# Gated scan with span products on rounded operands in two parts; delta inputs, gates and head norm in one block

## The reference

```
odn_x = _deltanet_scans(_dn_inputs(px[0], px[2], px[3], ...), _dn_inputs(pc[0], pc[2], pc[3], ...), ctx_out)
ohg_x = _hgrn2_scans(_hg_inputs(column-major px[4], px[5], px[6], lb), _hg_inputs(pc[4], pc[5], pc[6], lb), ctx_out)

def _dn_inputs(qkv, b, a, conv_w, a_log, dt_bias):
    qkv = silu(_short_conv(qkv, conv_w))
    q, k, v = split(qkv, 3)                      # 4 heads of 128 each
    q = _l2norm(q) * 128 ** -0.5 ; k = _l2norm(k)
    beta = sigmoid(b)
    g = -exp(a_log) * softplus(a + dt_bias)

gla_chunked, for each head and direction d, in chunks:
    gcum = cumsum(log_f)
    s_new = s * exp(g_last) + (k * exp(g_last - gcum))^T v
    att[i, j] = sum_k q[i, k] k[j, k] exp(gcum[i, k] - gcum[j, k])   for j <= i
    o = (q * exp(gcum)) s + att v
```

## Time and profile before

| quantity | value |
| --- | --- |
| device time, median of 3 (range) | 3605.03 us (3597.1 to 3607.6) |
| device time of the profiled execution | 3603.17 us |
| its span, first to last instruction | 3601.3 us |
| mean granted TensorE clock | 0.960 of 2.4 GHz |
| TensorE matmul busy | 3322.1 us (92%) |
| VectorE / ScalarE / GpSimd busy | 2266.4 / 1464.2 / 317.2 us |
| delta inputs, gates, head norm | 1955.3 to 2123.3 us of the span |
| gated scan | 2507.7 to 2661.3 us of the span |

### The profile page before, as it was taken

How to read it: one execution, slowest core, us unless ns; L and a number is a source line. 1 busy time by engine, 2 the same in 40 slices (tenths; PEclk the granted TensorE clock), 3 DMA queues, 4 the chain that set the end, 5 groups by cost and what they waited for, 6 DMA issues and landing times. The chain is left out here.

```text
span 3601.3 us, 46913 instructions
## 1 busy us (share of the span) xinstructions
PE 3322.1 (92%) x18718; PEld 2706.7 (75%) x18718; DVE 2266.4 (63%) x2960; ACT 1464.2 (41%) x1943; POOL 317.2 (9%) x213
## 2 busy tenths in 40 slices
PE   7998989999999998899998978889889989999996
PEld 5887678888887887777777858779667766777774
DVE  6467756656565237668686445665655337888885
ACT  5216713212123127533233333433333136777774
POOL 0020000000000000000000023411100012222221
PEclk8999989999999999999999979999989979999998
DMA  6540013443443211155652139012023258999993
GB/s 237 201 151 13 1 47 106 144 159 117 162 126 92 63 66 42 35 157 184 204 186 86 57 107 271 4 48 59 1 58 86 65 203 302 381 370 368 379 360 105
DMA packets 371768, 522.49 MB, mean 145 GB/s; under 512 B 19712, under 2 KB 313216, under 8 KB 345984
## 3 DMA queue, kind: packets, MB, share of 16 engines
q1 hardware_dynamic: 362112, 503.21, 41.8%
q0 software_dynamic: 9472, 16.80, 1.4%
HBM read 484.81 MB, written 51.90 MB: 149 GB/s over the span
## 5 line engine op out<-in xcount | busy, mean ns | idle before, releaser
L270 DVE TENSOR_TENSOR lo<-exp_raw,exp_hi 128x2048 fp32r<-128x2048 f32 x192 | 439.1, 2291 | 63.2 <-ACT exp_hi L3396 63.1
L3396 ACT CAST exp_hi<-exp_raw 128x2048 fp32r<-128x2048 f32 x192 | 366.5, 1913 | 112.7 <-PE exp_down_acc L265 50.7
L263 PE MATMUL ffn_acc<-normed_hi,up_w_hi 128*128 128x512 f32 (+1 forms) x1056 | 378.1, 358 | 9.6 <-DVE lo L626 6.1
L264 PE MATMUL ffn_acc<-lo,up_w_hi 128*128 128x512 f32 (+1 forms) x1056 | 377.9, 358 | 0.0
L263 PEld LDWEIGHTS ffn_acc<-normed_hi,up_w_hi 128*128 128x128 f32 x1056 | 199.9, 189 | 43.7 <-issue 6.7
L421 DVE SCALAR_TENSOR_TENSOR aside_w<-aside_w,aside_c 128x1024 f32<-128x1024 f32 x176 | 209.1, 1221 | 26.4 <-DMA aside_w<-in_ada_t 19.4
L264 PEld LDWEIGHTS ffn_acc<-lo,up_w_hi 128*128 128x128 f32 x1056 | 200.5, 190 | 32.1
L263 PE MATMUL ffn_acc<-gated_hi,down_w_hi 128*128 128x512 f32 (+1 forms) x528 | 190.8, 361 | 16.7 <-DVE lo L270 16.6
L1275 ACT ACTIVATE conv<-ffn_acc,vecs 128x768 f32<-128x768 f32 (+1 forms) x88 | 73.2, 882 | 292.6 <-PE ffn_acc L265 292.6
L265 PE MATMUL ffn_acc<-normed_hi,up_w_lo 128*128 128x512 f32 (+1 forms) x528 | 190.1, 360 | 0.0
L264 PE MATMUL ffn_acc<-lo,down_w_hi 128*128 128x512 f32 (+1 forms) x528 | 189.6, 359 | 0.0
(11 more groups left out here) (593 smaller groups left out, 8783.3 us busy)
## 6 DMA issues: line engine op xcount, KB each, us to landing
exp_raw<-in_w_experts SPq DMA_DIRECT2D x192, 1024.0 KB, 7.9
aside_w<-in_ada_t SPq DMA_DIRECT2D x176, 512.0 KB, 6.2
up_w<-in_ffn_up SPq DMA_DIRECT2D x88, 512.0 KB, 5.2
x_rows<-dn_zero SPq DMA_DIRECT2D x42, 384.0 KB, 5.3
y_rows<-dn_zero SPq DMA_DIRECT2D x42, 384.0 KB, 5.2
ada_w<-in_ada_first SPq DMA_DIRECT2D x8, 1024.0 KB, 12.1
v<-in_ada_t SPq DMA_DIRECT2D x16, 512.0 KB, 6.6
down_w<-in_ffn_down SPq DMA_DIRECT2D x16, 512.0 KB, 4.1
```

The source lines that it names most:

```text
L263: nc.tensor.matmul(out, left[0], right[0], start=start, stop=False)
L264: nc.tensor.matmul(out, left[0], right[1], start=False, stop=False)
L270: return engine.tensor_tensor(lo, value, hi.bitcast(F32), ALU.subtract)
L3396: nc.scalar.copy(hi[slot(e, j)][:], raw[tile(e, j)][:]).then_inc(tile_hi[j], 1)
```

## The change

**Delta inputs.** `dn_gates` and the call of `head_norm` for the delta inputs are gone; `dn_inputs` holds all three. TensorE makes chunks 0 to 7 (q and k), then the 48 products of the gates as a thirteenth item (n = 8) in the same ring of PSUM banks, then the chunks of v (n = 9 to 12). The sums of squares stand after the gates (chunks 0 to 3) and after n = 9 (4 to 7). The spreads of the roots stand inside n = 11 and n = 12 (0, 1, 2) and behind them (3 to 7). ScalarE's squares, exp, ln, sigmoid and root, and VectorE's reciprocal and scalings, stand between the steps of the chunks.

**Gated scan.** Each latent log gate is split into a rounded high part and a rounded rest. The high part lies in the context columns of `x` (two buffers), the rest over the gate in `fi`. Each span product, and each latent sum, is two `fp32r` matmuls in place of one float32 matmul. The tables are rounded once by GpSimd, `strict` by VectorE. The first head's gates are split at the end of `gated_rows` by VectorE; the next head's by a ScalarE copy ahead of the late exponentials, and a VectorE subtraction after level 1. Context sums stay float32.

```
+        sq = K.sb(ctx, "hn_sq", [P, HEADS, TT])
+        rstd = K.sb(ctx, "hn_rstd", [normed, TT])
+        root_hi = K.sb(ctx, "hn_root_hi", [normed, TT], FR)
+        root_lo = K.lo(rstd)
+        unit = K.sb(ctx, "hn_rows", [normed, normed], FR)
...
+        def bank(c):
+            return acc[:, {4: 1, 5: 2, 7: 1}[c]] if c in (4, 5, 7) else spread
...
+            def wide(n, between={}):
+                ring.begin(pe, n)
                 for c in range(KD):
...
+                    for a, b in parts:
+                        last = products(nc, acc[:, n % ACCS, a:b], ring.weights(n, c), right(c, a, b), c == 0, c == KD - 1)
+                    if c in between:
+                        stretch(between[c])
+                last.then_inc(ring.acc_full[n % ACCS], 1)
+            def gates():
+                pe.wait_ge(w_split, 1)
+                pe.wait_ge(ring.acc_free[gates_at % ACCS], gates_at // ACCS)
+                for a, b in parts:
+                    for c in range(KD):
+                        last = products(nc, acc[0:16, gates_at % ACCS, a:b], (wh[:, c, :], wl[:, c, :]), right(c, a, b),
+                                        c == 0, c == KD - 1)
+                last.then_inc(ring.acc_full[gates_at % ACCS], 1)
+            def turn_gates():
+                pe.wait_ge(rows_ready, 1)
+                for t in range(NT):
+                    last = nc.tensor.transpose(acc[:, gates_at % ACCS, TT + t * 16:TT + (t + 1) * 16], rows[:, t * P:(t + 1) * P], ident[0:16, 0:16])
+                last.then_inc(turned, 1)
+            def sums(some):
+                for c in some:
+                    pe.wait_ge(sq_full, c + 1)
+                    for a, b in parts:
+                        last = nc.tensor.matmul(spread[0:normed, a:b], pick[:, KD - 1 - c:KD - 1 - c + normed], sq[:, c % HEADS, a:b],
+                                                start=(c == 0), stop=(c == normed - 1))
+                    last.then_inc(summed, 1)
...
+            def stretch(c):
+                if c == 0:
+                    pe.wait_ge(split, 1)
+                elif c in (4, 5):
+                    pe.wait_ge(ring.acc_free[c - 3], (count + c - 4) // ACCS)
+                else:
+                    pe.wait_ge(scaled, {6: 4, 7: 5}.get(c, c))
+                row = unit[:, c:c + 1].broadcast_to([normed, P])
+                for a, b in parts:
+                    nc.tensor.matmul(bank(c)[:, a:b], row, root_hi[:, a:b], start=True, stop=False)
+                    last = nc.tensor.matmul(bank(c)[:, a:b], row, root_lo[:, a:b], start=False, stop=True)
+                last.then_inc(spread_full, 1)
+            ring.multiply(pe, acc, normed, first.ready, right, parts, inner_root)
+            gates()
+            pe.wait_ge(kept, 1)
+            sums(range(0, HEADS))
+            turn_gates()
+            wide(9)
+            sums(range(HEADS, normed))
+            wide(10)
+            wide(11, {5: 0})
+            wide(12, {1: 1, 5: 2})
+            for c in range(3, normed):
+                stretch(c)
...
+            def square(c):
+                if c >= HEADS:
+                    act.wait_ge(summed, c - HEADS + 1)
+                act.wait_ge(out[c % 2], c // 2 + 1)
+                nc.scalar.activation(sq[:, c % HEADS, :], dst[:, c, :], ACT.Square).then_inc(sq_full, 1)
...
+                if n == gates_at:
+                    for c in range(HEADS, normed):
+                        square(c)
+                    ring.high(act, n + 2)
+                    act.wait_ge(biased, 1)
+                    nc.scalar.activation(e[:], e[:], ACT.Exp)
+                    nc.scalar.activation(rate[:], K.row("a_log"), ACT.Exp)
+                    act.drain()
+                    nc.scalar.activation(l[:], e[:], ACT.Ln, bias=1.0)
+                    nc.scalar.activation(beta[:], beta[:], ACT.Sigmoid)
+                    act.drain()
+                    act.sem_inc(exped, 1)
...
+                if 1 <= n <= HEADS:
+                    square(n - 1)
+                if n == gates_at + 1:
+                    act.wait_ge(inverted, 1)
+                    nc.scalar.activation(rstd[:], rstd[:], ACT.Sqrt).then_inc(rooted, 1)
...
+            def take_gates():
+                ring.done(dve, gates_at)
+                nc.vector.tensor_copy(rows[:], acc[0:16, gates_at % ACCS, 0:TT]).then_inc(rows_ready, 1)
...
+            def bias_gates():
+                dve.wait_ge(turned, 1)
+                found = acc[:, gates_at % ACCS, TT:TT + NT * 16].rearrange("p (t n) -> p t n", n=16)
+                nc.vector.tensor_copy(beta[:], found[:, :, 0:8])
...
+            def scale(c):
+                dve.wait_ge(spread_full, c + 1)
+                nc.vector.scalar_tensor_tensor(dst[:, c, :], dst[:, c, :], P ** -0.5 if c < HEADS else 1.0,
+                                               bank(c)[:, 0:TT], ALU.mult, ALU.mult).then_inc(scaled, 1)
...
+            for n in range(count):
+                c = chunk[n]
+                if n == gates_at:
+                    take_gates()
+                    ring.low(dve, n + 2)
+                    bias_gates()
+                    continue
+                dve.wait_ge(mid[c % 2], c // 2 + 1)
...
+                if 4 <= n + 2 < count and n + 2 != gates_at:
+                    ring.low(dve, n + 2)
+                keep(n)
+                if n == gates_at + 1:
+                    dve.wait_ge(summed, normed)
+                    nc.vector.tensor_scalar(rstd[:], spread[0:normed, 0:TT], 1.0, EPS, ALU.mult, ALU.add)
+                    dve.drain()
+                    nc.vector.reciprocal(rstd[:], rstd[:]).then_inc(inverted, 1)
+                    finish_gates()
+                    dve.wait_ge(rooted, 1)
+                    nc.vector.tensor_copy(root_hi[:], rstd[:])
+                    dve.drain()
+                    lo_of(nc.vector, root_lo[:], rstd[:], root_hi[:]).then_inc(split, 1)
+                if n == gates_at + 2:
+                    scale(0)
+                    scale(1)
+                if n == gates_at + 3:
+                    scale(2)
+                    scale(3)
+            for c in range(4, normed):
+                scale(c)
+            dve.drain()
@@ gated_rows
+            def split_gates():
+                raw, hi, lo = gates
+                dve.wait_ge(unshifted, HEADS * P // G + 1)
+                nc.vector.tensor_copy(hi, raw).then_inc(gates_hi, 1)
+                dve.wait_ge(gates_hi, 1)
+                lo_of(nc.vector, lo, raw, hi)
...
             unshift(GATES - 1)
+            split_gates()
...
+def gate_parts(K, fi):
+    wide = lambda t, it: t[:, 0:NTX, 0:2 * HEADS * P].rearrange("p t (d h n) -> p t d h n", d=2, h=HEADS)[:, :, :, it, :]
+    own = lambda t, u: t[:, u * NTX:(u + 1) * NTX, TX:TT].rearrange("p t (d n) -> p t d n", d=2)
+    high, low = K.lo(K.x), K.lo(fi)
+    return [(wide(fi, it), own(high, it % 2), wide(low, it)) for it in range(HEADS)]
@@ hgrn
+        before = K.sb(ctx, "hg_strict", [P, 2, P], FR)
+        before_ready, spans_ready, gates_hi, gates_lo = (K.sem("hg_" + n) for n in ("strict", "spans_ready", "gates_hi", "gates_lo"))
+        masks_fr = K.lo(spans)
...
+            for part in range(2):
+                own = slice(part * EARLY * P, (part + 1) * EARLY * P)
+                pool.wait_ge(spans_full[part], 16)
+                nc.gpsimd.tensor_copy(masks_fr[:, :, own], spans[:, :, own]).then_inc(spans_ready, 1)
             for it in range(HEADS):
                 pool.wait_ge(ekd_ready, it + 1)
                 nc.gpsimd.tensor_tensor(kd[:, 0:NT, :], kk[:, :, it * P:(it + 1) * P], ekd[:, 0:NT, :],
...
-                nc.tensor.matmul(B[:, 6 + n % 2, :], column(fi, c, it + d * HEADS),
-                                 spans[:, d, part * EARLY * P:(part + 1) * EARLY * P], start=True, stop=True).then_inc(e_full, 1)
+                _, hi, lo = parts[it]
+                table = masks_fr[:, d, part * EARLY * P:(part + 1) * EARLY * P]
+                nc.tensor.matmul(B[:, 6 + n % 2, :], hi[:, c, d, :], table, start=True, stop=False)
+                nc.tensor.matmul(B[:, 6 + n % 2, :], lo[:, c, d, :], table, start=False, stop=True).then_inc(e_full, 1)
+            def latent_sums(it, d, lo, hi):
+                out = span(0, 3)[:, d * NT + lo:d * NT + hi, :]
+                _, high, low = parts[it]
+                nc.tensor.matmul(out, before[:, 1 - d, :], high[:, lo:hi, d, :], start=True, stop=False)
+                nc.tensor.matmul(out, before[:, 1 - d, :], low[:, lo:hi, d, :], start=False, stop=True)
...
+                if it == 0:
+                    pe.wait_ge(before_ready, 1)
+                else:
+                    pe.wait_ge(gates_lo, it)
                 for d in range(2):
-                    for lo, hi in ((0, 4), (4, 6)) if d == 0 else ((0, 2), (2, 6)):
-                        h = it + d * HEADS
-                        last = nc.tensor.matmul(span(0, 3)[:, d * NT + lo:d * NT + hi, :], strict[:, 1 - d, :],
```

(26 more changed lines are left out.)

193 lines of the change are left out of this document (84 added, 109 removed).

## The result

The changed kernel takes 3562.7 us (median of four runs, 3559.4 to 3564.2) for 3604.5 (3597.1 to 3607.6): a ratio of 0.9886, 95% interval 0.9869 to 0.9903. The forecast was 3564.0, range 3554 to 3576. The profiled execution took 3561.9, its span 3560.1 for 3601.3: 41.2 us less.

A forecast was written before the change was run, and what follows sets the result against it. TensorE was taken as the bound in the delta inputs' stretch and the scan's levels, VectorE in the scan's late chain. 3603.2 - 28.5 (part 1) - 10.7 (part 2) = 3564.0 us, range 3554 to 3576.

The forecast's parts named there:

- Part 1: Delta inputs: everything else fits beside TensorE's grown stream, the block ends at 2094.8 for 2123.3, 28.5 us less.
- the spreads: Delta inputs: spreads of the roots cost TensorE 0.70 us each, three inside n = 11 and 12, 2.1 in all.
- Rival 2: Delta inputs: chains don't fit beside the stream, TensorE stalls 6 to 12 us at n = 10 or 11; 3570 to 3576; chance 0.14.
- the margin at n = 10: Delta inputs: VectorE has the split ready about when TensorE ends n = 10, next convolution late by 0.2 us or less.
- Part 2: Gated scan: cheaper span products and sums save 15.2 us over four heads, less 4.5 for the clock: 10.7 us.
- the forecast's 1.5 for the clock: Gated scan: clock falls to half ahead of level 5, 1.5 us lost in each of three heads, 4.5 in all.
- the walk: Gated scan, one head step by step: it ends at 32.3 us for 36.2, 3.9 less, before any loss by the clock.
- The level's pace: Gated scan: a level takes TensorE 1.83 us, below VectorE's 1.97, so VectorE sets the pace, plus 1.2 after level 1.
- Rival 3: Gated scan: VectorE is the bound anyway, only 1 us per head stays; 3571; chance 0.07.
- Rival 1: The clock holds in the scan and at the delta net's opening, there 2.7 us more gained; 3556.8; chance 0.22.
- Rival 4: Gated scan: rounded products don't run at the rounded pace, two cost what one did; 3579; chance 0.04.
- Rival 5: Gated scan: clock falls in the first head and stays at half, 11 us more per head; 3619; chance 0.03.

The follow-up runs named there:

- the delta inputs alone: The kernel before with only the delta inputs, gates and norm put in one block, the gated scan as before: 3577.1 us, ratio 0.9925.
- the repetition: The changed kernel, unaltered, measured once more: 3565.4 us, ratio 0.9896, scan 137.3 us.
- the filled kernel: The changed kernel with eight rounded matmuls that nobody reads ahead of level 5 in heads 0 to 2: 3562.2 us, ratio 0.9891.
- the pauses half filled: The changed kernel with eight matmuls that nobody reads at the end of the delta inputs, three ahead of the last spread, five behind: 3567.3 us, ratio 0.9898.

## Why the prediction was right, step by step

**Part 1: 28.5 forecast, 27.4 measured.** At the block's end it was 26.2. The rest came in stages whose work is unchanged, and it is not this part's own: in the trace of the delta inputs alone, with the same 26.2 at the block's end, 29.3 had come of it at the scan. The walk held. The end of the chunk stream, taken at ScalarE's last convolution, came 23.8 us later for 21.3 forecast. Terms: gates 8.37 for 8.4; the sums 2 x 5.33 for 10.3, since their records start 0.33 apart and not 0.32; turning 0.54 and 0.2 to go back, for 0.5; 0.4 ahead of the fourth chunk, not forecast, of which 0.17 was there before the block began, while the other 0.3 fall where VectorE also splits the gates' weights (that this is the reason was not tried); and 0.3 since two chunks that took 8.21 before now take 8.35 like the others. **The step that was mis-sized is the spreads.** I priced one at 2 x 0.23 + 2 x 0.12 = 0.70. The rows above show it: from 2085.95 the next product would have followed at 2086.07, it came at 2087.04 and its successor 0.34 later for 0.23: 1.08. At each change between the two kinds of product the first start is 0.1 late and its successor another 0.1, which a price taken inside a stream leaves out. Three spreads: 3.3 for 2.1. The tail took 7.9 for 8.1 forecast. Rival 2 fell: the split was ready at 2069.3 for 2068.1 forecast, with 6 us of cover. One reading in it was wrong: the margin at n = 10, which the prediction put at 0.2 us, was 1.1. It compared the split with TensorE's end of n = 10, but VectorE's next task waits for ScalarE's copy of that chunk, another 0.90 us (the idle time of 1.12 ahead of 2070.41 above).

**Part 2: 10.7 forecast, 13.1 measured.** In the order of the heads, from first sum to first sum, and with the forecast's 1.5 for the clock taken off in the first three: 4.6 measured for 2.2, 2.4 for 2.4, 2.3 for 2.4, 4.2 for 3.7, and 0.3 lost at the start to VectorE's rounding of the matrix. In the repetition the scan is 1.9 us shorter still, by as much as its last head, where the clock was at half for 10 us and not 14; its first and third heads cancel. A gain of 13 or of 15 us is a matter of the execution. Three things in it:
- The clock. It fell ahead of level 5 as forecast in the second and third head, for 1.5 each; in the first it fell one pause earlier, and cost nothing. So the term was 3.0 for 4.5 in this execution, and 3.1 in the repetition (first and second head). By the rule of the Trainium skill that the prediction named (TensorE: Matmul & The Clock Gate, Why this matters for your kernels) all three heads pay; here the clock fell in all three, and two of them paid. That the fall, not something else, makes the difference is shown by the filled kernel's second head at full clock and by the repetition's third, where the fall lies ahead of level 4: both take 32.3 us, the number of the walk. The walk's pauses were a little long: 2.5 us ahead of level 5 and 1.5 ahead of level 4, for 3.1 and 1.8.
- The first head. GpSimd's rounding of a table took 1.04 and 1.11 for my 1.2, and the first span product starts 5.15 behind the first sum, for 4.56 before. But from there to the product behind the eight early ones it is 5.3 for 7.3, a gain of 2.0 where I had 1.6. Up to level 0 the head gained 2.2, in the levels 1.6, behind level 5 0.8: 4.6 without any loss by the clock, for 3.7.
- The level's pace. I said that VectorE sets it at 1.97, and put its added subtraction into the pace. In the last head, with no subtraction, the levels follow at 1.81 to 1.83, TensorE's 0.90 + 0.93; elsewhere at 1.82 to 1.9, once per head 2.49. The 1.97 was built from two starts and one duration, and the duration is longer than the distance to the next start (0.76 for 0.67): VectorE's own pace is 1.90. The levels of the last head gained 2.4 by it for 1.9 forecast; another 0.4 came at its end, where the clock was back for the last outputs. Rival 3 (VectorE the bound anyway, 3571) is wrong by the same rows.

Rival 1 at the opening of the delta net, 2.7 us for a clock that holds, didn't come true in any of the kernels, not even with the pauses half filled. Rival 4 fell: the two matmuls of a span product start 0.23 to 0.34 apart. Rival 5 fell: in the first three heads the clock was back within 4 us, and within 8 in every other kernel.

In sum the total was met to 1.3 us partly by luck: 1.1 too much in part 1 and 2.4 too little in part 2 cancel, and each of the two moves by 2 us between executions. What the forecast passed over is larger than either. It named the collision of `hg_qe` with VectorE's late product, said rightly that it stays, and took its 2.1 us per head as given; one added wait takes it away.

## What to carry to other kernels

Price a short group of matmuls that is put into a stream of another kind with its two changes (0.2 us each here), and take a pace from distances between starts, never from a duration. Ask of a thin margin which engine the next task really waits for. Where GpSimd and VectorE both multiply from SBUF, move the one with slack beside operations that read PSUM. Where TensorE stops being the bound, ask of each pause what stands behind it: a fall of the clock costs only where TensorE's work is next on the path. Moving work away from one gap to shorten another gained nothing here (a scan of 142.7 us for 137.3 and 139.2).
